# Delta-rule level products on 64-column tiles, with four moved waits and operations, in a two-block transformer kernel

## The reference

```python
def second_block(...):
    proj = rms_norm(x, g_mix) @ w_in          # q, k, v, z, f, scal (4 numbers a head), gates
    y_a = gated_deltanet_branch(q, k, v, z, scal, ...)   # conv of 5 taps, silu, l2 norm, delta rule both ways
    y_f = fourier_branch(f, w_fourier)
    x = x + (gate_a * y_a + gate_f * y_f) @ w_o
    ...

def gated_delta_rule_chunked(q, k, v, g, beta):      # 8 heads of 128, chunks of CHUNK = 64 tokens
    gc = cumsum of g within the chunk
    decay = where(i >= j, exp(gc_i - gc_j), 0)
    m = where(i > j, (k * beta) @ k.T * decay, 0)
    u, w = solve (I + m) [u, w] = [v * beta, k * beta * exp(gc)]     # unit lower triangular, 64 by 64
    qk = where(i >= j, q @ k.T * decay, 0)
    for each chunk:                                   # the state s runs over the 4 chunks
        v_new = u - w @ s
        o = (q * exp(gc)) @ s + qk @ v_new
        s = s * exp(gc_last) + (k * exp(gc_last - gc)).T @ v_new
```

## Time and profile before

| | |
|---|---|
| median of 3 runs | 3136.91 us |
| the profiled execution | 3135.63 us |
| its span, first to last instruction | 3133.8 us |
| TensorE busy | 3034.0 us, 97% |
| VectorE, ScalarE, GpSimd busy | 2009.5, 1404.7, 329.8 us |
| mean granted TensorE clock | 0.990 |

### The profile page before, as it was taken

How to read it: one execution, slowest core, us unless ns; L and a number is a source line. 1 busy time by engine, 2 the same in 40 slices (tenths; PEclk the granted TensorE clock), 3 DMA queues, 4 the chain that set the end, 5 groups by cost and what they waited for, 6 DMA issues and landing times.

```text
span 3133.8 us, 43317 instructions
## 1 busy us (share of the span) xinstructions
PE 3034.0 (97%) x14671; PEld 2507.5 (80%) x14671; DVE 2009.5 (64%) x2655; ACT 1404.7 (45%) x1764; POOL 329.8 (11%) x306
## 2 busy tenths in 40 slices
PE   8999899999999999999989999999999999999997
PEld 7878678887888888887868877778777888888886
DVE  5755766656667776667568656666555666666665
ACT  6444444454444444445544533333544444444443
POOL 0004950000000000000000243223000000000000
PEclk9999999999999999999999999999999999999999
DMA  6554333356555555553565523333565555555554
GB/s 217 175 184 161 126 116 133 122 188 210 189 183 187 187 189 192 188 183 129 190 200 173 172 81 105 109 100 107 169 218 190 183 189 187 190 188 188 189 183 134
DMA packets 145705, 525.79 MB, mean 168 GB/s; under 512 B 16416, under 2 KB 17184, under 8 KB 144864
## 3 DMA queue, kind: packets, MB, share of 16 engines
q1 hardware_dynamic: 140416, 504.25, 49.0%
q0 software_dynamic: 1600, 12.04, 1.1%
q10 hardware_dynamic: 3616, 8.52, 0.8%
HBM read 516.36 MB, written 8.39 MB: 167 GB/s over the span
## 4 chain that ended last, share of the span: by engine, by line
PE 69%; issue 24%; POOL 3%; DVE 2%; ACT 1%; DMA 1%; DVEq 0%; POOLq 0%; SPq 0%; ACTq 0%
PE bank L1956 20%; PE bank L1958 19%; PE bank L1957 19%; PE bank L2346 1%; PE bank L2338 1%; PE bank L2054 1%; PE bank L2352 1%; PE bank L1981 1%; ACT w_hi L728 1%; POOL xs L569 0%; PE bank L2207 0%; PE bank L2452 0%; PE bank L2181 0%; PE bank L2250 0%; DMA dft_t_sb<-c_dft_t 0%
## 5 line engine op out<-in xcount | busy, mean ns | idle before, releaser
L1226 DVE TENSOR_TENSOR w_lo<-w_raw,w_hi 128x1024 fp32r<-128x1024 f32 x952 | 1194.6, 1265 | 862.5 <-ACT w_hi L728 860.2
L728 ACT CAST w_hi<-w_raw 128x1024 fp32r<-128x1024 f32 x952 | 998.7, 1052 | 1430.1 <-PE bank L1958 1409.1
L1956 PE MATMUL bank<-w_hi,a_hi 128*128 128x512 f32 x2816 | 1125.8, 400 | 16.3 <-DVE w_lo L1226 13.6
L1958 PE MATMUL bank<-w_hi,a_lo 128*128 128x512 f32 x2816 | 1102.6, 392 | 0.0
L1957 PE MATMUL bank<-w_lo,a_hi 128*128 128x512 f32 x2816 | 1101.4, 391 | 0.0
L1956 PEld LDWEIGHTS bank<-w_hi,a_hi 128*128 128x128 f32 x2816 | 532.0, 189 | 133.4 <-issue 14.8
L1958 PEld LDWEIGHTS bank<-w_hi,a_lo 128*128 128x128 f32 x2816 | 531.5, 189 | 113.7
L1957 PEld LDWEIGHTS bank<-w_lo,a_hi 128*128 128x128 f32 x2816 | 532.6, 189 | 108.8 <-issue 3.8
L1956 PE MATMUL bank<-w_hi,m_hi 128*128 128x512 f32 x512 | 200.3, 391 | 5.1 <-DVE m_lo L1902 5.1
L531 POOL TENSOR_TENSOR rstd<-rstd,neg_half 128x2 f32<-128x2 f32 x7 | 5.5, 785 | 1882.6 <-DVE rstd L1255 1882.6
L1957 PE MATMUL bank<-w_lo,m_hi 128*128 128x512 f32 x512 | 200.1, 391 | 0.0
(11 more groups left out here) (387 smaller groups left out, 2597.1 us busy)
## 6 DMA issues: line engine op xcount, KB each, us to landing
w_raw<-weights SPq DMA_DIRECT2D x952, 512.0 KB, 4.0
gate<-gate_st ACTq DMA_DIRECT2D x8, 512.0 KB, 3.8
h<-gate ACTq DMA_DIRECT2D x8, 512.0 KB, 5.0
gain<-gains POOLq DMA_DIRECT2D x3, 1024.0 KB, 8.7
h<-x_tok SPq DMA_DIRECT2D x4, 512.0 KB, 10.3
w_proj_sb<-w_proj POOLq DMA_DIRECT2D x1, 2048.0 KB, 9.7
h_rest<-h POOLq DMA_DIRECT2D x1, 2048.0 KB, 12.7
h<-h_rest POOLq DMA_DIRECT2D x1, 2048.0 KB, 8.3
```

The costliest lines, as they stand in the source:

```text
L728: nc.scalar.copy(w_hi[:, s, :], w_raw[:, s, :]).then_inc(hi_ready, 1)
L1226: V.tensor_tensor(w_lo[:, s, :], w_raw[:, s, :], w_hi[:, s, :].bitcast(F32), ALU.subtract).then_inc(lo_ready, 1)
L1956: T.matmul(psum[t][:], left_hi[:, ts], wh, start=first, stop=False)
L1958: last = T.matmul(psum[t][:], left_lo[:, ts], wh, start=False, stop=final)
```

## The change

Five things are changed.

- `by_chunk` replaces one matmul of 128 by 128 by 128 by two of 64 stationary and 64 moving columns, one for each diagonal block, in `level_z`, `level_rz` (both products) and in the k k and k q products (L2405).
- GpSimd makes `vb`, `kb` and `kd` of both heads at the head of a turn, after a new wait for `dn_free`; `eT` moves from level 1 to level 2, `qd` from level 1 to level 3.
- Gate slab 3 stands between the transposes of the first head and those of the second.
- The narrow weights are rounded after the split of quad `Q_QKV2 + 2` and the copy of the first result, and wait for seven loads; `dft_t` is counted in `h_moved`, whose waits go up by one load.
- `masked_scores` stands after `updates(3)`.

```diff
@@ GpSimd
             pool.dma_start(h_rest, h[:]).then_inc(h_moved, 16)
-            pool.dma_start(dft_t[:], const["dft_t"]).then_inc(small3_loaded, 16)
+            pool.dma_start(dft_t[:], const["dft_t"]).then_inc(h_moved, 16)
             pool.wait_ge(pair_free[0], 2 * (U_F + 1) + 2)
-            pool.wait_ge(h_moved, 16)
+            pool.wait_ge(h_moved, 2 * 16)
...
+                pool.wait_ge(dn_free, heads[1].of(i))
+                for hd in heads:
+                    nc.gpsimd.tensor_tensor(hd.vb, tokens(2 * DNW, hd.x), of_head(beta, hd.x), ALU.mult)
+                    nc.gpsimd.tensor_tensor(hd.kb, tokens(DNW, hd.x), of_head(be, hd.x), ALU.mult)
+                    nc.gpsimd.tensor_tensor(hd.kd, tokens(DNW, hd.x), of_head(kd, hd.x), ALU.mult).then_inc(dn_in, 1)
                 for k in range(1, LEVELS):
...
                     for hd in heads:
-                        if k == 1:
+                        if k == 2:
                             pool.wait_ge(dn_eT, hd.of(i))
                             nc.gpsimd.tensor_tensor(hd.eT, hd.eT, cums, ALU.mult).then_inc(dn_eTm, 1)
+                        elif k == 3:
                             pool.wait_ge(dn_egb, hd.of(i))
...
-                        elif k == 2:
-                            nc.gpsimd.tensor_tensor(hd.vb, tokens(2 * DNW, hd.x), of_head(beta, hd.x), ALU.mult)
-                        elif k == 3:
-                            nc.gpsimd.tensor_tensor(hd.kb, tokens(DNW, hd.x), of_head(be, hd.x), ALU.mult)
-                        elif k == 4:
-                            nc.gpsimd.tensor_tensor(hd.kd, tokens(DNW, hd.x), of_head(kd, hd.x), ALU.mult).then_inc(dn_in, 1)
@@ ScalarE
             late_operand(Q_QKV2, TR_MIX2, C_MIX2, lambda: squares(h, qkv2, DC - 1, gated, TT * DC))
-            act.wait_ge(small3_loaded, 8 * 16)
-            nc.scalar.copy(s_hi[:], s_raw[:]).then_inc(narrow_hi_ready, 1)
             q = Q_QKV2
             split(q + 2)
             act.wait_ge(slab_done, QUAD * (q + 2))
             root_of(N_MIX2)
             scaled(s_stage[:, 0, 0, :], pair[0][0][:], N_MIX2, 0).then_inc(pair_free[0], 1)
+            act.wait_ge(small3_loaded, 7 * 16)
+            nc.scalar.copy(s_hi[:], s_raw[:]).then_inc(narrow_hi_ready, 1)
@@ VectorE
             late_operand(Q_QKV2, TR_MIX2, C_MIX2, N_MIX2)
-            dve.wait_ge(narrow_hi_ready, 2)
-            V.tensor_tensor(s_lo[:], s_raw[:], s_hi[:].bitcast(F32), ALU.subtract).then_inc(narrow_lo_ready, 1)
             q = Q_QKV2
             split(q + 2)
             dve.wait_ge(slab_done, QUAD * (q + 2))
             root_of(N_MIX2)
             scaled(s_stage[:, 0, 1, :], pair[0][1][:], N_MIX2, 1).then_inc(pair_free[0], 1)
-            dve.wait_ge(small3_loaded, 8 * 16)
+            dve.wait_ge(narrow_hi_ready, 2)
+            V.tensor_tensor(s_lo[:], s_raw[:], s_hi[:].bitcast(F32), ALU.subtract).then_inc(narrow_lo_ready, 1)
+            dve.wait_ge(small3_loaded, 7 * 16)
...
                 updates(2)
-                masked_scores()
                 split(q + 2, 1, 2)
                 updates(3)
+                masked_scores()
@@ TensorE
+                def by_chunk(out, left, right):
+                    for c in range(P // CHUNK):
+                        r = slice(c * CHUNK, (c + 1) * CHUNK)
+                        last = T.matmul(out[r, r], left[:, r], right[:, r], start=True, stop=True)
+                    return last
...
-                            last = T.matmul(hd.at(2, n), hd.mk[:, t, d], hd.r[:, t, d], start=True, stop=True)
+                            last = by_chunk(hd.at(2, n), hd.mk[:, t, d], hd.r[:, t, d])
...
-                            last = T.matmul(hd.at(2, n), hd.t[:, t, d], hd.zz[:, t, d], start=True, stop=True)
+                            last = by_chunk(hd.at(2, n), hd.t[:, t, d], hd.zz[:, t, d])
...
-                                last = T.matmul(hd.at(0, n), hd.zz[:, t, d], hd.t[:, t, d], start=True, stop=True)
+                                last = by_chunk(hd.at(0, n), hd.zz[:, t, d], hd.t[:, t, d])
...
-                            last = T.matmul(hd.at(1, TT * (1 - a) + t), hd.qk[:, 1, ts], hd.qk[:, a, ts], start=True, stop=True)
+                            last = by_chunk(hd.at(1, TT * (1 - a) + t), hd.qk[:, 1, ts], hd.qk[:, a, ts])
...
                         last = T.transpose(hd.at(2, n), hd.t[:, t, d], ident[:])
                     last.then_inc(dn_rT, 1)
-                gate_slab(3)
+                    if hd.x == 0:
+                        gate_slab(3)
```

More of the change, by code:

```diff
@@ L1072, in _ @@
             act.wait_ge(slab_done, QUAD * (q + 2))
-            act.wait_ge(h_moved, 16)
+            act.wait_ge(h_moved, 2 * 16)
             scaled(fr[:, 0, NC:], pair[1][0][:], N_MIX2, 0).then_inc(pair_free[1], 1)
@@ L1713, in _ @@
             dve.wait_ge(slab_done, QUAD * (q + 2))
-            dve.wait_ge(h_moved, 16)
+            dve.wait_ge(h_moved, 2 * 16)
             scaled(fr[:, 1, NC:], pair[1][1][:], N_MIX2, 1).then_inc(pair_free[1], 1)
@@ L1882, in _ @@
             rest_of_operand(TR_WO2)
-            dve.wait_ge(h_moved, 2 * 16)
+            dve.wait_ge(h_moved, 3 * 16)
             project_into_h(Q_WO2, TR_MLP, C_MLP, N_MLP)
```

## The result

The kernel after takes 3112.3 us (median of 4 runs, 3106.08 to 3114.93), the kernel before 3135.93 beside it (4 runs, 3134.69 to 3137.34): a ratio of 0.9918, interval 0.9905 to 0.993. It is faster by 23.6 us, half of the 47.1 forecast, and above the range. The profiled execution took 3113.68 us.

A forecast was written before the change was run, and what follows sets the result against it. TensorE, busy 97% of 3133.8 us, was taken as the bound. 4 x (2.0 + 6.15 + 0.65) - 1.5 = 33.7, plus 13.4, gives 47.1; 3136.9 - 47.1 = 3090 us, forecast 3083 to 3100, with rivals to 3107.

The forecast's parts named there:

- The tiles: Delta-loop levels 2 to 4: a product falls from 0.22 to 0.11 us, saving 6.15 us a turn.
- Late rounding: Second block's start: the 13.04 us TensorE wait and cold clock go, 15.4 us less 2 for lateness: 13.4 us.
- Tiles and switches: Delta-loop levels: 0.055 us a pair of passes, 0.34 a switching round trip; a level saves 2.05 of 8.13 us.
- D: Rival on tiled products: pairs don't overlap, only the switches' cost is left, 3133 us; chance 0.05.
- E: Rival on tiled products: a pass has a floor of its own, so the kernel is slower, 3149 us; chance 0.05.
- A turn: One of four delta-loop turns: saves 2.0 at the head, 6.15 in levels 2 to 4, 0.65 in the tail.
- Tail: Level 5 at a turn's end: 3.15 us with hops against 3.8 before, 0.65 us a turn saved.
- Feeders: VectorE and GpSimd in the levels: they follow at 6.1 us a level; cost 0, bound 1 us a turn.
- rival B: Levels 2 and 3: GpSimd or VectorE sets their pace, 15 us less gain, 3105 us; chance 0.12.
- Head: Start of a turn: the wait moves to `level_z(1)`, `level_rz(1)` starts 0.85 us earlier; 2.0 us a turn saved.
- Clock: Delta loop: the lower clock is expected again after a rest of 2.8 us, costing 1.5 us in all.
- rival C: Delta-loop levels: the clock falls as TensorE's columns are half as busy, costing 16 us, 3106; chance 0.08.

The follow-up runs named there:

- e2: The kernel after with TensorE's four delta-loop turns written out instead of a loop, other engines unchanged: 3091.81 us, ratio 0.9858.
- e10: The written-out kernel (e2) with gate slab 3 back behind the transposes of both heads: 3093.05 us, ratio 0.9862.
- e1: The kernel before with only the late narrow rounding (parts around `s_hi`, `s_lo`, `dft_t`): 3122.37 us, ratio 0.9954.
- e9: The written-out kernel (e2) with GpSimd's list in the order of the kernel before: 3092.43 us, ratio 0.9862.
- e3: The kernel after with every product back at full width, all the moves kept: 3124.18 us, ratio 0.9957.
- e4: The kernel after with tiles in the z products alone, other products full width: 3118.26 us, ratio 0.9944.
- e6: The kernel after with tiles only in z and the product for r, not in t, k k and k q: 3114.49 us in one run.
- e8: The written-out kernel (e2) with both r copies before the exponentials, and level 1's `zz` copies and updates before the splits: 3077.58 us, ratio 0.9817.
- e5: The kernel after with each product as two passes of 64 moving columns on full-width weights, no tiles: 3254.68 us in one run.

## Why the prediction was wrong

The step that failed stands in "The tiles" and in the sum behind it: a product "becomes four passes, two pairs: 0.11 us instead of 0.22", and four times (2.0 + 6.15 + 0.65) was taken as what a turn saves. Each pass was priced by its stream, its weight load and the switch, and the turn as their sum. That the loop's body grows by 480 instructions, and must be there again after each jump back, was not looked at, and no rival named it: each rival with tiles was about how passes run. The before trace held the clue: instruction packets in the first turn alone, so the other three ran on what was there.

What the jumps cost is e2 against the kernel after, 20.5 us of the 23.5 that are missing: at the jump before the third turn, starts lie 3.6 us apart where e2 has 0.6, and 2.6 where six passes take 0.2, so some 5.4 us of rest. TensorE's waits by what released them, in the whole loop (1800 to 2160 us) of the kernel after, with us in total, times, longest:

```profile
PE bank L2406 <- issue: 8.6, 3, 3.1
...
PE bank L2335 <- issue: 2.8, 2, 2.2
```

That is 11.4 us of rest. The rest of the price is passes at 1.2 GHz behind it, and the traces show how much. From the last state update (L2401) of a turn to the next turn's first transposes (L2420), the kernel after takes 18.64, 19.53 and 20.23 us and e2 each time 12.94 or 12.95. The third turn's transposes, in e2 at 1979.97 as shown under e10:

```profile
1994.22 0.66 PE L2420 MATMUL bank<-ident_sb,delta 128*128 128x128 f32 x4 [0.43 <-DVE delta L1807]
```

The three jumps differ by 19.6 us in all, 11.4 of rest and some 8 of slower passes; behind the first transposes the third turn runs alike in both. The remaining 3 us are within the medians' spread and the sizes of the terms below.

**Late rounding:** right. Forecast 13.4; 14.5 by e1, 12.5 by the traces.

**Tiles and switches:** right in mechanism and nearly in size. One level's tiled groups take 1.09 + 2.01 = 3.10 us from the first tiled start to the slab behind, and 3.28 with the 0.09 at each way in; the forecast, with the way in, was 3.14. A level saves 1.85 us, forecast 2.05. The pair is 0.060 us, close to the lower bound that I took (0.055), far from 0.109. The Trainium skill's rule of the drain ("TensorEngine Tiling (Array Packing)", Key Properties) stands, and its price is about as forecast: the tiles start 0.31 to 0.33 us behind the slab's last pass, 0.09 over the usual 0.225, and the first group is left 0.13 us later than its sixteen pairs of 0.060 end, where the prediction had 0.09 and 0.155. Rivals D and E fell with the level of 6.28 us.

**A turn:** in e2 the second takes 84.04 us against 91.98, 7.9 saved where 8.8 less 0.4 of clock was forecast; the third takes 84.96, 7.0 saved. From the loop's first row sums to the Fourier mixer's first pass, e2 saves 31.8 us of the 33.7 forecast and the kernel after 12.5. From the median 3136.9 the forecast was 3090, and e2 gives 3091.8. So the sum was right to some 2 us for a kernel whose instructions are there, and e2 is not the kernel that was asked about. That it fits so closely is in part luck: the late rounding gave more by e1's median than its term, and the loop and the stretch behind it less.

**Tail:** from z of level 5 to the products for u and w the third turn takes 3.26 us, forecast 3.15, before 3.81.

**Feeders:** TensorE doesn't rest in levels 2 to 4 (rival B fell). The step that called GpSimd's old order "too late for an earlier level 2" was wrong: e9 has the same time.

**Head:** the wait moved from the second transposes to the second z, 2.61 us where 2.7 were forecast. But the 0.85 us that `level_rz(1)` should have started earlier, 3.4 us in four turns, didn't show: e10 has it undone and is 1.2 us slower, where single runs of either kernel lie up to 4.7 apart, and in e3 the moves bring nothing. Whether they are worth a microsecond stays open.

**Clock (rival C):** it fell, but not in the levels, where it is 1.00; it fell behind rests, at the jump and in the head. The forecast had 1.5 us for this. After the loop the lead shrank too, from 25.1 to some 22 us, where the Fourier mixer's stretch from 2161 to 2190 us ran at 0.88 (the same stretch of the kernel before, 2184.5 to 2213, at 1.00); why it did there wasn't tried. It isn't the reload or the tiles: e2 and e3 take as long over its first group of passes (5.3 and 5.4 us, before 3.7).

Not settled: whether the limit between 99 and 109 KB is one of bytes or of which 16 KB pieces the body touches. Counted in pieces from the start of TensorE's list, the body touches 6 pieces before, 7 in e4 and e6, and 8 in the kernel after; 8 and one loaded ahead would be the nine packets a turn. No run moved the body without changing its length, so this is a guess.

## What to carry to other kernels

Before splitting instructions inside a hardware loop, count the body's instructions on that engine, and look when the instruction queue is active in the trace: if it is silent in the later turns, the body is being reused, and an edit that makes it loud must pay for a rest at each jump. If the body must be long, write out the loop on that engine alone (here some 20 us for one line). Leaving one product unsplit kept the body short too, but gave nothing here: its lost gain and the further switches between tiled and full-width products cost as much as the jumps (e6, 3114.49 us). So where products stand side by side, tile all of them or none. And when a wait moves to the next instruction, look for what stands ahead of its supplier's queue: there lay the 14 us of e8, which the slab's place could not reach.

## What the runs showed of the hardware

**Instruction loads.** Bodies of 78, 89 and 99 KB on TensorE were loaded once (before, e4, e6); bodies of 109 KB (the kernel after, e5) were loaded again in each turn, eight or nine packets of 16 KB a turn, with a rest of 2.6 to 3.3 us at the jump. In the kernel after, two of three jumps had a second rest, of 2.2 and 0.7 us, six passes into the first group behind the row sums. The Trainium skill, "Runtime: NRT & Kernel Launch", Instruction fetch mechanics, says that instructions arrive in blocks of 16 KiB and that loading runs ahead only in straight order; packets of 16.4 KB and e2 without a rest at the turns agree. It also says that a taken branch out of "the current 2-page window" waits for a fetch of its target. The rests at the kernel after's jumps agree with the wait, but not with the window: bodies of 78 to 99 KB, five to six packets of 16.4 KB, were jumped back in without a rest. It gives TensorE 128 KiB; a body of 109 KB would fit into that and still was loaded again, so here a loop could not count on all of it.

**A pair of passes on two column tiles** takes 0.109 us with 128 moving columns and 0.060 with 64: the stream's halving is nearly all passed on. Going into the tiles and out again costs 0.34 us (e6).
